# Expert rows in a one-by-one order, and the bias tables' transfers issued two stages earlier

## The chip, the cores and the metric

The kernel runs on one core of a Trainium2 chip. The core has five engines with a queue of instructions each: TensorE (PE, with its weight loads as PEld), VectorE (DVE), ScalarE (ACT), GpSimd (POOL) and SyncE (SP). They run side by side and meet only at semaphores. Sixteen DMA engines move data between HBM and the core's memory for all of them. The metric is the device time of one execution in microseconds (us), the median over runs.

## The reference: what is computed

One inference step of a two-layer backbone. 128 context tokens and 512 latent tokens, 1024 channels each, are five blocks of 128 tokens (block 0 is the context). For each layer:

```
sh1, sc1, g1, sh2, sc2, g2 = modulation(cond, w_ada, b_ada)
outs = token_mixer(x * (1 + sc1) + sh1, p)         # 12 attention heads in three groups, and a gated MLP
x = layer_norm(ALPHA * x + g1 * merge_groups(outs, ...), ...)
x = layer_norm(ALPHA * x + g2 * peer_ffn(x * (1 + sc2) + sh2, p), ...)
```

`peer_ffn` routes each token, in each of 8 heads, to 16 of 16384 experts. For one head `h` and slot `k`:

```
act = gelu(peer_u[eid] . x)                        # a "u row": 1024 numbers for each token, a dot product
out += gate * act * peer_v[eid]                    # a "v row": 1024 numbers for each token, a weighted sum
```

That is 8 x 16 u rows and as many v rows for each block of tokens, 256 in all, each a gather of 128 x 4 KB = 512 KB from HBM. Five blocks in two layers make 2560 gathers. Attention group B adds a bias by 2-D offset (`nat_rpb`), for which the kernel builds a table in HBM once, before the first latent block.

## The kernel before, in words

The program is a row of stages with a barrier of all engines between them (`end_step`, L370): `step_modulation` (M), `step_input` (I, one block), `step_attend_route` (A, one block). Layer 0 goes M, I0, A0, I1 to I4, A1 to A4; layer 1 the same, and two closing stages. The expert work of a block is spread over later stages, beside their own work: `Experts(L, block, first, heads)` is a share of it. Six A stages (A2, A3 and A4 of each layer) carry a full block, 8 heads and so 256 rows; the last block's 256 rows have a stage of their own near the end (`step_experts_only`). The other stages carry 1 to 5 heads.

**The order of the rows** is one list that all engines walk (`row_order`, L67): first the 16 u rows of head 0, then `turn` u rows and `turn` v rows by turns. The v rows of head h come about one head after its u rows. `turn` is SHORT_TURN = 4 for a full block and 16 for a smaller share. A row goes through these hands:
- POOL gathers row r into slot r % 8 of the ring, once row r - 8 has been used (`gather_until`, L493). POOL issues strictly in the order of the list.
- A u row: DVE takes its dot product with the token (L594). After u row 15 of a head ACT does the gelu of 16 sums (L529); DVE makes the weights `wsel` of the head's v rows from it (L587), just ahead of v row 0.
- An odd v row: DVE adds it to `acc` (L604). An even v row: ACT writes the weight on a diagonal (L536, four buffers), PE multiplies by it into PSUM (L562, on record as four matmuls). `on_pe` (L80) decides.

**Where rows stand in a stage's own work** is set by shares: each engine calls `rows(n)` between pieces of its own work, which carries it to row n of the list. In an A stage, attention head i of 12 stands between `rows(9 i)`, `rows(9 i + 4)` and `rows(9 i + 9)`. In half i, rows 9 i to 9 i + 3 stand right before the head's value products (PE, L1157), for which DVE waits before it scales the result (L1326). DVE's `rows` come before that wait, PE's before those products. Then follow the projection `w_out` (PE L1169, DVE L1360), the routing's projection (PE L1189) and its top 16 (DVE, L1375 to L1390).

**The bias tables** are `bias_rows_gpsimd` (L631), called by POOL at the start of stage A0: 16 transfers from HBM to HBM, which lay out the rows (L638), a wait for them, two loads of the tables into the unused ring (L643), a wait, two additions of the mask (L647), two stores (L650). Behind them in POOL's queue stands the power function for the group norm of A0's attention result (L1273), for which DVE waits (L1355). No expert rows run in M, I0 and A0 of layer 0, so POOL has little to do there.

Of the kernel before, what the change touches and what calls it, by code (L numbers as in the profile page):

```python
# [16 lines left out]
DEPTH, D = 2, 1024  # L17
# [16 lines left out]
PH, PK, TOPK = 8, 128, 16  # L34
# [24 lines left out]
HEAD_ROWS = 2 * TOPK  # L59
BY_PE = 2  # L60
DIAGS = 4
SHORT_TURN = 4

# [8 lines left out]
def row_order(heads, turn):  # L74


    u = [("u", h, k) for h in range(heads) for k in range(TOPK)]
    v = [("v", h, k) for h in range(heads) for k in range(TOPK)]
    order, u = u[:TOPK], u[TOPK:]
    while v:  # L80
        order += u[:turn] + v[:turn]
        u, v = u[turn:], v[turn:]
    return order


def on_pe(kind, k):
    return kind == "v" and k % BY_PE == 0


class Experts:  # L90
# [7 lines left out]
    def __init__(self, layer, block, first, heads, begin=False, end=False, ended=None):  # L98
        self.layer, self.block, self.first, self.heads = layer, block, first, heads
        self.begin, self.end, self.ended = begin, end, ended  # L100
        self.order = row_order(heads, SHORT_TURN if heads == PH else TOPK)

        self.by_dve, self.by_pe = [], []
        d = p = 0
        for kind, _, k in self.order:
            if on_pe(kind, k):
                p += 1
            else:
                d += 1
            self.by_dve.append(d)  # L110
            self.by_pe.append(p)

        self.before = block * PH + first + layer * (NBLK * PH)
# [10 lines left out]
def build(nc, a):  # L124
    es = ExitStack()
    with es:
# [5 lines left out]
        def sem(name):  # L132
            s = es.enter_context(nc.semaphore(name))
            sems.append(s)
            return s
# [150 lines left out]
        pieces_used = sem("pieces_used")  # L286
# [6 lines left out]
        const_in = sem("const_in")  # L293
# [78 lines left out]
        def chain(eng, s):  # L372

            n = [0]

            def link(ins):
                n[0] += 1
                ins.then_inc(s, 1)
                eng.wait_ge(s, n[0])
            return link  # L380
# [54 lines left out]
        def last_sum_rstd(pool):  # L435
            pool.wait_ge(end_var, 1)
            pool.tensor_tensor(rstde[:, :], vee[:, :], neg_half[:, 0:1], ALU.pow).then_inc(end_rstd, 1)
# [7 lines left out]
        def experts_gpsimd_ended(pool, E):  # L445
            if E is not None and E.ended is not None:
                last_sum_rstd(pool)
# [174 lines left out]
        natmask = x2e[:, 0:GRID_W]  # L622
# [5 lines left out]
        def start_sync_more(sp):  # L628
            sp.dma_start(iota16[:, :], a["c_iota"]).then_inc(cache_in, 16)

        def bias_rows_gpsimd(pool):  # L631

            pool.dma_start(natmask, a["c_natmask"]).then_inc(const_in, 16)
            for l in range(DEPTH):
                for h in range(H):
                    for half in range(2):
                        first = ((l * H + h) * (2 * NA_KH - 1) + 1 - half) * RPB_ROW + RPB_PAD + NA_KW - 1
                        pool.dma_start(toep_dram[l, half * GRID_W:(half + 1) * GRID_W, h * NDR * GRID_W:(h + 1) * NDR * GRID_W]  # L638
                                       .rearrange("p (r c) -> r p c", c=GRID_W),
                                       bass.AP(a["rpb"].tensor, first, [[RPB_ROW, NDR], [-1, GRID_W], [1, GRID_W]])).then_inc(bias_stored, 16)  # L640
            pool.wait_ge(bias_stored, 16 * DEPTH * H * 2)
            for l in range(DEPTH):
                pool.dma_start(toepf[l], toep_dram[l, :, :]).then_inc(const_in, 16)  # L643
            pool.wait_ge(const_in, 16 * (1 + DEPTH))
            for l in range(DEPTH):
                t = toepf[l].rearrange("p (r c) -> p r c", c=GRID_W)
                pool.tensor_tensor(t, t, natmask.unsqueeze(1).broadcast_to([P, H * NDR, GRID_W]), ALU.add).then_inc(const_done, 1)  # L647
            pool.wait_ge(const_done, DEPTH)
            for l in range(DEPTH):
                pool.dma_start(toep_dram[l, :, :], toepf[l]).then_inc(bias_stored, 16)  # L650
# [6 lines left out]
        def step_modulation(L, E, first=False):  # L657
# [10 lines left out]
            with nc.Block() as block:  # L668
# [84 lines left out]
                @block.gpsimd  # L753
                def _(pool):
                    rows, finish = experts_gpsimd(pool, E)
                    experts_gpsimd_ended(pool, E)
                    for c in range(ADA_PIECES):
                        rows((c + 1) * SHARE)
                    finish()
# [30 lines left out]
        def step_input(L, b, context, weights, E):  # L790
# [4 lines left out]
            with nc.Block() as block:  # L795
# [129 lines left out]
                @block.gpsimd  # L925
                def _(pool):
                    link = chain(pool, pool_chain)
                    rows, finish = experts_gpsimd(pool, E)

                    def rope(out, src, nh, stride, half, first, tabs):  # L930

                        w = 2 * half
                        s4 = src.rearrange("p (h n) -> p h n", h=nh)
                        o4 = out.rearrange("p (h n) -> p h n", h=nh)
                        t4 = ropeA[:, 0:nh * w].rearrange("p (h n) -> p h n", h=nh)
                        u4 = ropeB[:, 0:nh * w].rearrange("p (h n) -> p h n", h=nh)
                        cos = rope_t[:, tabs:tabs + w].unsqueeze(1).broadcast_to([P, nh, w])
                        sin = rope_t[:, tabs + w:tabs + 2 * w].unsqueeze(1)
                        pool.tensor_tensor(u4, s4[:, :, first:first + w], cos, ALU.mult)
                        pool.tensor_tensor(t4[:, :, 0:half], s4[:, :, first + half:first + w],  # L940
                                           sin[:, :, 0:half].broadcast_to([P, nh, half]), ALU.mult)
                        link(pool.tensor_tensor(t4[:, :, half:w], s4[:, :, first:first + half],
                                                sin[:, :, half:w].broadcast_to([P, nh, half]), ALU.mult))
                        return pool.tensor_tensor(o4[:, :, first:first + w], u4, t4, ALU.add)

                    rows(96)

                    pool.wait_ge(var_done, 1)
                    pool.tensor_tensor(rstd[:, 1:3], ve[:, 1:3], neg_half[:, 0:2], ALU.pow).then_inc(rstd_done, 1)

                    pool.wait_ge(xT_done, 1)
                    pool.wait_ge(z_act, 1)
                    pool.wait_ge(loaded2, 16)
                    rope(kr[:, NOPE:CH], z[:, C_C + QR + KVR:C_D], 1, CH, ROPE // 2, 0, 0).then_inc(rope_done, 1)
                    pool.wait_ge(rope_done, 1)
                    pool.wait_ge(z_dve, 2)
                    rope(zr, z[:, C_D:C_D + 6 * HD], 6, HD, HD // 2, 0, 2 * ROPE).then_inc(rope_done, 1)
                    pool.wait_ge(rope_done, 2)
                    rows(144)

                    pool.wait_ge(var_done, 2)
                    pool.tensor_tensor(rstd[:, 0:1], ve[:, 0:1], neg_half[:, 0:1], ALU.pow).then_inc(rstd_done, 1)
                    rows(176)
                    pool.wait_ge(up_sb, 1)
                    rope(qc, qc, H, CH, ROPE // 2, NOPE, 0).then_inc(qc_roped, 1)
                    finish()

                @block.vector
# [65 lines left out]
        def step_attend_route(L, b, context, weights, E):  # L1034
# [48 lines left out]
            with nc.Block() as block:  # L1083
# [177 lines left out]
                @block.gpsimd  # L1261
                def _(pool):
                    rows, finish = experts_gpsimd(pool, E)
                    if E is None:
                        bias_rows_gpsimd(pool)
                    for i in range(NH):
                        if i == 1:
                            rows(HEAD_MID)
                            experts_gpsimd_ended(pool, E)
                        rows(i * HEAD_SHARE)  # L1270
                    rows(A_END)
                    pool.wait_ge(var_done, 1)
                    pool.tensor_tensor(rstd[:, :], ve[:, :], neg_half[:, :], ALU.pow).then_inc(rstd_done, 1)  # L1273
                    rows(TAIL[0])
                    rows(TAIL[2])
                    pool.wait_ge(var_done, 2)
                    pool.tensor_tensor(rstd[:, 0:1], ve[:, 0:1], neg_half[:, 0:1], ALU.pow).then_inc(rstd_done, 1)
                    for i in range(12):
                        rows(ROUTE[i])
                    if E is None:  # L1280
                        pool.wait_ge(bias_stored, 16 * (DEPTH * H * 2 + DEPTH))
                    finish()
# [320 lines left out]
```

## Time and profile before

| | us |
|---|---|
| median of 3 runs | 5437.8 (5434.72 to 5450.85) |
| profiled execution, its own time | 5450.89 |
| its span in the trace | 5449.1 |
| busy in the span: PE, DVE, POOL, ACT | 3095.8, 3441.4, 2880.5, 630.1 |
| bytes moved | 1664.83 MB, mean 306 GB/s |
| stages (start to start): M, I0, A0 of layer 0 | 107, 52, 208 |
| one full-block A stage | about 471 |

Engines overlap, so busy times do not add up to the span. A stage lasts until its slowest chain is through, since all engines meet at its end. In the rows of waits an arrow names what an engine waited for, and the numbers are the sum, the number of times and the longest.

### The profile page before, as it was taken

The page shows a single profiled execution, that of the slowest core. Times are in us where ns is not written, and L with a number is a line of the kernel's source. Part 1 is how long each engine was busy: PE and PEld are TensorE (multiplying, and loading weights), DVE is VectorE, ACT ScalarE, POOL GpSimd, SP SyncE. Part 2 cuts the span into 40 slices and gives each one's busy share as a digit, 9 for nine tenths or more (in the row PEclk, how much of TensorE's full clock was granted, in tenths as well). Part 3 has the DMA queues.
Part 4 walks back from the last instruction along what each step waited for, and adds up shares of the span by engine and source line. Part 5 has one row for each costly group of instructions (what it writes and reads, how often), then busy time and mean ns, then how long its engine had stood idle before and what let it go on. Part 6 is the DMA issues. An engine that isn't in the chain of part 4 may idle for free. (4 is left out here: it accounts for less than half of the span.)

```text
span 5449.1 us, 35111 instructions
## 1 busy us (share of the span) xinstructions
PE 3095.8 (57%) x9560; PEld 1601.3 (29%) x9560; DVE 3441.4 (63%) x6877; ACT 630.1 (12%) x1577; POOL 2880.5 (53%) x2837
## 2 busy tenths in 40 slices
PE   8446756357455635656555576645664664565454
PEld 2233334134122323411232233422332331232111
DVE  1245556666776856773468455566686677769665
ACT  0100120110021111000010001111111101211000
POOL 0216635366555645654455464435664564666675
PEclk9678858678677767878777787776776786777677
DMA  7537778789888988989888778778998898998998
GB/s 275 184 155 259 243 285 298 277 309 359 325 301 332 344 301 298 367 333 388 306 311 288 292 242 300 267 260 301 340 341 312 298 367 301 326 341 331 356 385 321
DMA packets 438101, 1664.83 MB, mean 306 GB/s; under 512 B 52928, under 2 KB 66304, under 8 KB 427376
## 3 DMA queue, kind: packets, MB, share of 16 engines
q0 software_dynamic: 370528, 1353.39, 67.7%
q1 hardware_dynamic: 67392, 309.32, 14.8%
q8 instruction: 78, 1.28, 0.1%
q14 instruction: 103, 0.84, 0.0%
HBM read 1634.85 MB, written 33.95 MB: 306 GB/s over the span
## 5 line engine op out<-in xcount | busy, mean ns | idle before, releaser
L562 PE MATMUL ps<-ring,diag 128*128 128x512 f32 x2560 | 1559.6, 759 | 1217.4 <-ACT diag L536 786.8
L493 POOL DMA_INDIRECT ring<-in_peer_v,eid_s x1280 | 1365.5, 1067 | 1038.3 <-PE ps L562 444.8
L493 POOL DMA_INDIRECT ring<-in_peer_u,eid_s x1280 | 1339.2, 1046 | 875.3 <-DVE dots L594 529.3
L594 DVE CUSTOM_DVE_ANT_0 ring<-ring,ps 128x1024 f32<-128x1024 f32 x1104 | 1305.8, 1217 | 121.1 <-DMA ring<-in_peer_u,eid_s 110.2
L562 PEld LDWEIGHTS ps<-ring,diag 128*128 128x128 f32 x2560 | 581.9, 242 | 2050.9 <-issue 1338.1
L604 DVE SCALAR_TENSOR_TENSOR acc<-ring,wsel,acc 128x1024 f32<-128x1024 f32 x640 | 827.1, 1292 | 486.0 <-DMA ring<-in_peer_v,eid_s 438.7
L852 PE MATMUL ps<-W,hT 128*128 128x512 f32 (+1 forms) x800 | 321.6, 563 | 31.2 <-DVE hT L978 22.0
L536 ACT ACTIVATE diag<-ident,wsel 128x128 f32<-128x128 f32 x640 | 225.2, 395 | 706.6 <-DVE wsel L587 392.2
L1189 PEld LDWEIGHTS ps<-hT,W 128*128 128x128 f32 x2560 | 294.7, 193 | 32.3 <-issue 17.7
L1189 PE MATMUL ps<-hT,W 128*128 128x128 f32 x2560 | 296.8, 277 | 11.6 <-ACT hT L1245 11.6
L594 DVE CUSTOM_DVE_ANT_0 ring<-ring,x2e 128x1024 f32<-128x1024 f32 x176 | 219.2, 1281 | 87.1 <-DMA ring<-in_peer_u,eid_s 85.9
L1137 PE MATMUL ps<-ktB,xs 64*128 64x512 f32 x64 | 49.3, 1130 | 316.3 <-DMA xs<-spill_state 179.5
L852 PEld LDWEIGHTS ps<-W,hT 128*128 128x128 f32 x800 | 150.5, 202 | 191.3 <-issue 166.0
L735 PE MATMUL ps<-W,condS 128*2 128x512 f32 x384 | 173.4, 612 | 41.1 <-DMA toep<-in_b_ada 41.1
L1300 DVE SCALAR_TENSOR_TENSOR big<-ps,toep 128x512 f32<-128x512 f32 x32 | 22.0, 689 | 256.4 <-DMA band<-in_c_band 213.9
L1152 PE MATMUL ps<-ident,big 128*128 128x128 f32 x504 | 107.1, 353 | 133.6 <-ACT big L1228 133.6
L484 POOL COPY eid_s<-eid_e 128x16 uint32<-128x16 uint32 (+1 forms) x80 | 17.9, 224 | 298.7 <-DMA eid_e<-expert_ids 211.5
L529 ACT ACTIVATE gel<-dots 128x16 f32<-128x16 f32 x80 | 17.2, 216 | 1362.8 <-DVE dots L594 1316.8
L1326 DVE TENSOR_SCALAR aux<-ps,small 128x64 f32<-128x64 f32 x120 | 34.1, 284 | 188.9 <-PE ps L1157 186.7
L1169 PE MATMUL ps<-W,hT 128*128 128x512 f32 x320 | 142.2, 600 | 1.1 <-ACT hT L1240 1.1
L1152 PEld LDWEIGHTS ps<-ident,big 128*128 128x128 f32 x504 | 81.5, 184 | 183.1 <-ACT big L1228 142.5
L1235 ACT COPY big<-ps 128x512 f32<-128x512 f32 x96 | 56.3, 586 | 597.3 <-PE ps L1152 597.3
(206 smaller groups left out, 2848.6 us busy)
## 6 DMA issues: line engine op xcount, KB each, us to landing
W<-in_w_q SPq DMA_DIRECT2D x28, 2048.0 KB
W<-in_w_ada SPq DMA_DIRECT2D x24, 2048.0 KB
W<-in_w_out SPq DMA_DIRECT2D x10, 4096.0 KB, 27.0
W<-in_w_in SPq DMA_DIRECT2D x16, 2048.0 KB, 8.1
ring<-in_peer_u,eid_s POOLq DMA_INDIRECT x1280, 6.3
ring<-in_peer_v,eid_s POOLq DMA_INDIRECT x1280, 6.1
toep<-mod_rows SPq DMA_DIRECT2D x20, 512.0 KB, 7.6
aux<-mod_rows SPq DMA_DIRECT2D x19, 512.0 KB, 5.9
```

What stands on the lines that cost most here:

```text
L493: pool.indirect_dma_start(ring[:, r % RING, :], None, a["peer_u"] if kind == "u" else a["peer_v"], bass.IndirectOffsetOnAxis(ap=eid_s[:, h ...
L536: act.activation(diag[:, n % DIAGS, :], ident[:, :], ACT.Copy, scale=wsel[:, h % 2, k:k + 1]).then_inc(diag_done, 1)
L562: last = pe.matmul(acc_ps[:, c * 512:(c + 1) * 512], diag[:, (E.by_pe[r] - 1) % DIAGS, :], ring[:, r % RING, c * 512:(c + 1) * 512], start ...
L594: dve.tensor_tensor_reduce(out=ring[:, r % RING, :], in0=ring[:, r % RING, :], in1=x2, scale=1.0, scalar=0.0, op0=ALU.mult, op1=ALU.add, a ...
L604: dve.scalar_tensor_tensor(acc[:, :], ring[:, r % RING, :], wsel[:, h % 2, k:k + 1], acc[:, :], ALU.mult, ALU.add).then_inc(used_dve, 1)
L735: last = pe.matmul(bank(c % NB, parts=2), condS[:, k, :], ada[:, c % NB, k, :], start=(k == 0), stop=(k == KD - 1))
L852: last = pe.matmul(bank(c, n), hT[:, k, :], w_in[c][:, k, :], start=(k == 0), stop=(k == KD - 1))
L1137: pe.matmul(near(i, lat), q, k[:, k0 * P:k0 * P + lat], start=True, stop=True)
L1152: last = pe.transpose(into, pr[:, i % 2, s * P:(s + 1) * P], ident[:, :])
L1169: last = pe.matmul(bank(2 + c), hT[:, k, :], w_out[:, k, c * 512:(c + 1) * 512], start=(k == 0), stop=(k == KD - 1))
L1189: last = pe.matmul(bank(2 + i % 2)[:, g * P:(g + 1) * P], w_q[c][:, k, g * P:(g + 1) * P], hT[:, k, :], start=(k == 0), stop=(k == KD - 1))
L1235: act.copy(prT[:, i % 2, 0:lat], near(i, lat))
```

## The change

Two things. In a full block the two kinds of row alternate one by one behind the first 16 (`turn` 1 for 4). And `bias_rows_gpsimd` is cut in three: the 16 transfers are issued in the first modulation stage once 8 of its 12 weight pieces have been used; the mask's load, the wait for the 16, and the table loads go to the front of POOL's queue in I0, with the wait for these at its end; the additions and stores stay at the start of A0.

```
-SHORT_TURN = 4
...
-        self.order = row_order(heads, SHORT_TURN if heads == PH else TOPK)
+        self.order = row_order(heads, 1 if heads == PH else TOPK)
...
-        def bias_rows_gpsimd(pool):
-
-            pool.dma_start(natmask, a["c_natmask"]).then_inc(const_in, 16)
+        def bias_rows_begin(pool):
+
+            pool.wait_ge(pieces_used, 8)
             for l in range(DEPTH):
                 for h in range(H):
                     for half in range(2):
...
                         pool.dma_start(toep_dram[...], bass.AP(a["rpb"]...)).then_inc(bias_stored, 16)
+
+        def bias_rows_load(pool):
+
+            pool.dma_start(natmask, a["c_natmask"]).then_inc(const_in, 16)
             pool.wait_ge(bias_stored, 16 * DEPTH * H * 2)
             for l in range(DEPTH):
                 pool.dma_start(toepf[l], toep_dram[l, :, :]).then_inc(const_in, 16)
-            pool.wait_ge(const_in, 16 * (1 + DEPTH))
+
+        def bias_rows_end(pool):
+
             for l in range(DEPTH):
...
                     experts_gpsimd_ended(pool, E)
+                    if first:
+                        bias_rows_begin(pool)
...
+                    if E is None:
+                        bias_rows_load(pool)
                     rows(96)
...
                     rope(qc, qc, H, CH, ROPE // 2, NOPE, 0).then_inc(qc_roped, 1)
+                    if E is None:
+                        pool.wait_ge(const_in, 16 * (1 + DEPTH))
                     finish()
...
                     if E is None:
-                        bias_rows_gpsimd(pool)
+                        bias_rows_end(pool)
```

**POOL, first stages.** In the program before, POOL's queue at the start of A0 of layer 0:

```order
L1261 UNCONDITIONAL_BRANCH
L633 DMA x2e<-in_c_natmask 128x64
L638 DMA bias_rows<-in_rpb 14x64x64 x16
L643 DMA ring<-bias_rows 128x3584 x2
L647 TENSOR_TENSOR ring<-ring,x2e 128x3584 x2
L650 DMA bias_rows<-ring 128x3584 x2
L1273 TENSOR_TENSOR rstd<-ve,neg_half 128x4
```

Now, from the first modulation stage into I0 (the row `L369 ISA` is the barrier between them), up to the first power function of I0:

```order
L637 DMA bias_rows<-in_rpb 14x64x64 x16
L673 UNCONDITIONAL_BRANCH
L369 ISA
L932 UNCONDITIONAL_BRANCH
L643 DMA x2e<-in_c_natmask 128x64
L646 DMA ring<-bias_rows 128x3584 x2
L958 ISA
L958 TENSOR_TENSOR rstd<-ve,neg_half 128x2
```

And at the start of A0, now:

```order
L1272 UNCONDITIONAL_BRANCH
L652 TENSOR_TENSOR ring<-ring,x2e 128x3584 x2
L655 DMA bias_rows<-ring 128x3584 x2
L1284 TENSOR_TENSOR rstd<-ve,neg_half 128x4
L1288 TENSOR_TENSOR rstd<-ve,neg_half 128x1
```

The small transfers left A0 for M, the table loads left it for I0; ahead of A0's first power function stand two additions and two stores.

**ACT, a full-block A stage**, around the gelu of expert head 1 and the exponentials of attention heads 6 and 7. Before:

```order
L536 ACTIVATE diag<-ident,wsel 128x128 x2
L529 ACT_TABLE_LOAD
L529 ACTIVATE gel<-dots 128x16
L536 ACTIVATE diag<-ident,wsel 128x128
L1226 ACT_TABLE_LOAD
L1226 ACTIVATE big,small<-ps,small 128x512
```

Now:

```order
L535 ACTIVATE diag<-ident,wsel 128x128
L528 ACT_TABLE_LOAD
L528 ACTIVATE gel<-dots 128x16
L535 ACTIVATE diag<-ident,wsel 128x128 x2
L1237 ACT_TABLE_LOAD
L1237 ACTIVATE big,small<-ps,small 128x512
```

Before, the diagonal behind the gelu is that of v row 12 of head 0. Now all diagonals of head 0 stand ahead of the gelu, and the two behind it are v rows 0 and 2 of head 1.

**DVE, the same stage**, in attention head 9, at the weights of expert head 2 (`wsel`), up to the scaling of the attention result. Before:

```order
L594 ISA ring,dots<-ring,ps 128x1024
L594 ISA dots 128x1
L594 ISA ring,dots<-ring,ps 128x1024
L594 ISA dots 128x1
L594 ISA ring,dots<-ring,ps 128x1024
L594 ISA dots 128x1
L594 ISA ring,dots<-ring,ps 128x1024
L594 ISA dots 128x1
L587 TENSOR_TENSOR wsel<-gel,gates_e 128x16
L1323 TENSOR_TENSOR small<-small 128x1
L1324 RECIPROCAL small<-small 128x1
L1326 TENSOR_SCALAR aux<-ps,small 128x64
```

Now:

```order
L603 SCALAR_TENSOR_TENSOR acc<-ring,wsel,acc 128x1024
L593 ISA ring,dots<-ring,ps 128x1024
L593 ISA dots 128x1
L586 TENSOR_TENSOR wsel<-gel,gates_e 128x16
L593 ISA ring,dots<-ring,ps 128x1024
L593 ISA dots 128x1
L603 SCALAR_TENSOR_TENSOR acc<-ring,wsel,acc 128x1024
L593 ISA ring,dots<-ring,ps 128x1024
L593 ISA dots 128x1
L1334 TENSOR_TENSOR small<-small 128x1
L1335 RECIPROCAL small<-small 128x1
L1337 TENSOR_SCALAR aux<-ps,small 128x64
```

The weights came last before the scaling, behind four dot products; now three rows of DVE's own stand between the weights and the scaling.

## Rows read from the trace of the kernel before

The rows of busy time (Rows 1 and 6) give the stretch and its length, then the busy time of each engine with its count of instructions, then PE's granted clock as a share of full speed, the DMA engines' busy share and the rate.

**Rows 1.** I0, A0, A, experts alone: PE, PEld, DVE, ACT, POOL; clock, DMA, GB/s.
```profile
107.00:159.00 52.00, 39.52 (x125) 20.98 (x125) 10.48 (x35) 5.56 (x11) 7.00 (x14) 0.86 0.23 72
159.00:367.00 208.00, 75.92 (x396) 57.93 (x396) 76.57 (x288) 17.44 (x52) 33.01 (x25) 0.62 0.38 141
1460.50:1932.00 471.50, 256.80 (x824) 137.46 (x824) 331.62 (x655) 61.74 (x152) 270.37 (x267) 0.75 0.88 324
...
5281.00:5321.00 40.00, 20.04 (x30) 7.66 (x28) 27.59 (x39) 2.88 (x9) 30.83 (x31) 0.74 1.01 378
```

**Rows 2.** POOL in order of time, I0 and A0 (start, length; in brackets idle before).
```profile
134.07 0.71 POOL L949 TENSOR_TENSOR rstd<-ve,neg_half 128x2 f32<-128x2 f32 x1 [133.62 <-DVE ve L993]
...
160.78 12.14 POOL L638 DMA_DIRECT2D bias_rows<-in_rpb  x15
207.16 0.82 POOL L638 DMA_DIRECT2D bias_rows<-in_rpb  x1 [34.24 <-issue]
...
222.85 15.41 POOL L647 TENSOR_TENSOR ring<-ring,x2e 128x3584 f32<-128x3584 f32 x2 [10.80 <-DMA ring<-bias_rows]
...
239.68 1.05 POOL L1273 TENSOR_TENSOR rstd<-ve,neg_half 128x4 f32<-128x4 f32 x1
```

**Rows 3.** Waits in the first 330 us (sum, times, longest).
```profile
DVE aux L1355 <- POOL rstd L1273: 30.3, 1, 30.3
...
DVE aux L1348 <- DMA xs<-in_x: 14.0, 1, 14.0
```

**Rows 4.** DMA queues of A0: 159 to 212 us, then 212 to 222.
```profile
q1 hardware_dynamic: 1840, 12.65, 61.5%
q0 software_dynamic: 1312, 3.71, 24.8%
...
q0 software_dynamic: 283, 3.67, 95.4%
```

**Rows 5.** SP in M: the last weight piece, the last load.
```profile
68.90 0.35 SPq L676 DMA_DIRECT2D W<-in_w_ada  x1
...
104.22 0.32 SPq L712 DMA_DIRECT2D modr<-mod_rows  x1
```

**Rows 6.** Busy time in M, 85 to 100 us, columns as in Rows 1.
```profile
85.00:100.00 15.00, 11.33 (x27) 2.12 (x25) 1.36 (x2) 0.00 (x0) 0.00 (x0) 0.99 0.84 314
```

**Rows 7.** Waits of DVE in a full-block A stage, 1460 to 1932 us.
```profile
DVE aux L1326 <- PE ps L1157: 25.2, 7, 5.1
```

**Rows 8.** DVE in attention heads 5 to 9 of that stage.
```profile
1586.34 0.28 DVE L1326 TENSOR_SCALAR aux<-ps,small 128x64 f32<-128x64 f32 x1 [5.03 <-PE ps L1157]
...
1602.72 0.28 DVE L1326 TENSOR_SCALAR aux<-ps,small 128x64 f32<-128x64 f32 x1 [4.55 <-PE ps L1157]
...
1629.36 0.28 DVE L1326 TENSOR_SCALAR aux<-ps,small 128x64 f32<-128x64 f32 x1
...
1647.18 0.28 DVE L1326 TENSOR_SCALAR aux<-ps,small 128x64 f32<-128x64 f32 x1 [5.06 <-PE ps L1157]
```

**Rows 9.** PE in that stage (four matmuls are one v row).
```profile
1606.78 1.98 PE L562 MATMUL ps<-ring,diag 128*128 128x512 f32 x4 [0.40 <-DMA ring<-in_peer_v,eid_s]
...
1642.37 3.52 PE L562 MATMUL ps<-ring,diag 128*128 128x512 f32 x4 [4.16 <-ACT diag L536]
...
1746.53 3.75 PE L562 MATMUL ps<-ring,diag 128*128 128x512 f32 x4 [13.67 <-ACT diag L536]
```

**Rows 10.** DVE behind the attention heads of that stage.
```profile
1718.59 1.23 DVE L1360 TENSOR_TENSOR aux<-ps,aux 128x1024 f32<-128x1024 f32 x1 [2.82 <-PE ps L1169]
...
1752.23 1.28 DVE L604 SCALAR_TENSOR_TENSOR acc<-ring,wsel,acc 128x1024 f32<-128x1024 f32 x1 [6.44 <-DMA ring<-in_peer_v,eid_s]
```

**Rows 11.** POOL's gathers by line, full-block A stage (busy, mean ns | idle before).
```profile
L493 POOL DMA_INDIRECT ring<-in_peer_v,eid_s x128 | 135.2, 1056 | 108.0 <-PE ps L562 50.7 <-issue 25.0 <-DVE acc L604 22.5
L493 POOL DMA_INDIRECT ring<-in_peer_u,eid_s x128 | 131.3, 1026 | 75.8 <-DVE dots L594 45.7 <-issue 26.2 <-POOL eid_s L484 2.1
```

**Rows 12.** Waits of POOL in the experts-only stage, 5070 to 5430 us.
```profile
POOL ring L493 <- issue: 70.1, 229, 0.5
```

## The prediction

> **What bounds the kernel now.** I read the table of busy times by stage first, since all engines meet at each stage's end and an average over the span hides that the stages have different limits. The reader sees three kinds [rows 1]. In M the DMA engines are busy 0.84 of the time near its end [rows 6]. In A0 nothing is busy: 208 us with a DMA share of 0.38. The full-block A stages last 471 us at a DMA share of 0.88, with DVE busy 332 of 471 us; where the experts run alone the DMA share is 1.0. So the order of the rows can win only in the six full-block A stages, from the 12% in which the DMA engines rest, 0.12 x 471 = 57 us in each.
>
> Second I read POOL's timeline and the waits in A0. POOL issues 15 of the small transfers in 12.14 us, then stands 34.2 us before the 16th, waits for the table loads, adds the mask for 15.4 us, and only then comes to the power function [rows 2]. DVE waits 30.3 us for that, with nothing else to do, and 14.0 us just before for a load of x that is late in a full queue [rows 3]. This is on the path that sets the stage's end.
>
> Third I read the waits of one full-block A stage. DVE idles 25.2 us in 7 of 12 attention heads for PE's value products [rows 7]. POOL idles 50.7 us until PE has used a slot of the ring, 45.7 us for dot products and 22.5 us for sums [rows 11].
>
> **The bias part, A0.** What goes from POOL's queue there: 16 issues, two waits, two loads. What stays ahead of the power function are the additions, 15.4 us, and the issue of two stores; begun at 160, that is over before 180. DVE asks for the function at 239.7 + 1.05 - 30.3 = 210.4 [rows 2, 3], so the 30.3 us go whole. What is late next is the load of x. In A0 the hardware queue used 61.5% of 53 us, 32.6 us of all 16 engines, and the small transfers 24.8%, 13.1 us. The latter go; the stores, of the size of the table loads (3.67 MB, 95.4% of 10 us, 9.5 us), now fall into this stretch [rows 4]. From 160.5 that makes 160.5 + 32.6 + 9.5 = 202.6. x came in a few short DVE operations ahead of 210.4, at about 208.7, so 6 us later than that. Gain: 30.3 + 6 = 36 us; ends: 25 (the additions slow down beside DVE's heads and the stores delay x) and 44.3 (both waits whole).
>
> **The bias part, M and I0.** The 16 transfers start when piece 8 is used, at about 69 us, where SP's own trigger stands [rows 5]. From there to 104 the queue of weights uses 0.84 of the engines [rows 6], 0.84 x 35 = 29.4 us; with 13.1 it is 42.5 us of work in 35, so 7.5 us too much. All of it delays M only if the weights pay; part falls into I0, where the DMA share is 0.23 [rows 1]. The lower end is 0. The upper end is the stand before the 16th issue: if it is again 34.2 us, POOL reaches M's barrier at 69 + 12.1 + 34.2 + 0.8 = 116.1, against I0's start at 107 [rows 1, 2], so 9 us. I take 5. Behind POOL's new wait in I0 stand the power function and the rotations, first wanted at 134 [rows 2]; the transfers are through by 116 in any case, and the table loads take 10 us in an idle DMA. I0 costs 0. The bias part in sum: -36 + 5 = -31 us (ends -44 and -16).
>
> A rule speaks against this move. The Trainium skill, DMA: Bandwidth & Descriptors, Queues, rings and completion order, says that each DMA engine takes packets from its queues by turns. Were those turns of equal time, the small transfers would be through after 13.1 / 0.5 = 26 us, well before M's end, and all of the 7.5 us would fall on the weights instead of 5. The trace shows 61.5 to 24.8 in A0, not equal time [rows 4]. By the rule the part would come to -28.5.
>
> **The order, what it costs on each engine.** Nothing is added. In 8 rows DVE has 4 dots and 2 sums in either order, and every sum waits for the DVE row before it in either; PE has 2 rows in either. What moves is where they stand.
>
> *Attention heads.* With turns of four, the four rows before a head's value products hold 0, 1 or 2 PE rows; now exactly 1, with 3 for DVE. A PE row takes 1.98 us at the full clock and 3.5 to 3.75 us at the lower one [rows 9], a DVE row up to 1.28 [rows 10]. The waits follow this: at 1629.36, four u rows and no PE row, DVE does not wait. The three near 5 us, 14.6 of the 25.2, have a further cause [rows 8]. Head 5: the diagonals of v rows 12 and 14 stand behind the gelu, which needs u row 15. Heads 6 and 9: v row 0's weights come behind four dots, and DVE has little or nothing left while ACT, PE and the products follow. The first cause is gone in the new order. For head 9 the 5.06 us hold that whole chain, with a PE row of 3.52. In the new order DVE has three rows, 3.7 us, beside it: a wait of 1.4, and none at the full clock, for 5.06. Against it: v row 0 of head 0 is now the last row of the half before, with a further PE row to follow, and head 6 has three PE rows; I count 4 to 5 us of wait in each of these two, and 1 us in each of five or six others at the lower clock. That is 15 us where 25.2 were: -10. DMA and ring give back half, since a DVE that is sooner meets rows that have not landed. I take -5 per stage; ends: -25 (all waits gone) and +17 (below).
>
> *Behind the heads.* PE stands 13.67 us for a diagonal behind a gelu; the slot comes free late, and DVE then waits 6.44 us for the v row that lands late [rows 9, 10]. In the new order these diagonals stand ahead of the gelu: -4 of the 6.4. Against that, the last PE row before each half of `w_out` is now the sixth of eight, not the third: 3 rows later, at 256 rows in 471 us up to 5.5 us. DVE waits 2.82 us there already [rows 10], so part of it counts: +3. In the top 16, DVE is busy nearly all the time and its work is the same: 0.
>
> Per stage -5 - 4 + 3 = -6, in six stages -36. The experts-only stage: POOL's main idle time is 229 gaps of 0.3 us between two issues, for which no row in use is to blame, and the DMA share is 1.0 [rows 1, 12]: 0, ends -5 and +3. The small shares keep turns of 16: 0.
>
> **The sum.** 5450.9 - 31 - 36 = 5383.9 for an execution like the profiled one, whose span of 5449.1 is all but 1.8 us of its time. It lies 13.1 us above the median of the runs, 5437.8, within their spread. Against the median: 5437.8 - 67 = 5371.
>
> **The rivals.**
> - *The order moves nothing (0.28).* The A stages carry 256 rows of 0.5 MB and some 18 MB beside them at a DMA share of 0.88; if the idle DMA time is that of chains which do not touch rows (start of stage, norms), only the bias counts: 5437.8 - 31 = 5407. For it: POOL's waits are short and many. Against it: the near 5 us waits recur in all six stages.
> - *The order wins far more (0.12).* If the 50.7 us for PE's slots [rows 11] mostly go and DMA fills them, -20 per stage: 5437.8 - 31 - 120 = 5287. Against it: the bytes of a stage in 20 us less would need a DMA share of 0.88 x 471 / 451 = 0.92 on average, start and norms included.
> - *Slower: PE at the lower clock sets the head (0.12).* Now each head has a PE row right before its products. The granted clock of the stage is 0.75 on average; if it falls with PE's work spread more evenly, each costs 3.5 to 3.75 us, and the five heads without a wait get one of 3.4 us: +17 per stage, 5437.8 - 31 + 102 = 5509. It decides when more than half of the PE rows in the heads take over 3 us; at +5 per stage the kernel is where it was.
> - *The bias part gives nothing (0.03).* If M ends 9 us later, I0 waits for the 16th transfer, and x stays late, some 15 us are left: 5437.8 - 15 - 36 = 5387. It moves the time little.
> - The forecast, in a broad sense (-2 to -14 per stage): 0.45.
>
> **How the numbers follow.** The forecast's own range is 5437.8 - 44 - 84 = 5310 to 5437.8 - 16 - 12 = 5410. I cut half of the far rival below and most of the slower one: 5302 to 5436. A measurement of this kernel can tell about 0.3%, 16 us, from no change. Below 5421 lie the forecast, the far win, the rival without bias and most of the one in which the order moves nothing; 0.8. Within 16 us lie the milder cases of the slower rival, where a loss of 3 to 8 us per stage eats the bias part, and the weak end of the neutral one: 0.11. Slower needs more than +8 per stage: 0.09.
>
> **What would show it.** A0: the wait of DVE L1366 (before: L1355) for the power function gone, the stage near 172 us for 208; the wait for x a few us shorter. M: 107 to 116 us, I0 as before, 52. Full-block A: about 465 us for 471; DVE's waits for value products 15 us for 25, none over 5 at head 5; PE's wait of 13.67 gone, DVE's wait at the projection longer than 2.82. Experts alone: as before. I am wrong if the A stages are longer than 471, if PE's granted clock falls below 0.7 there, or if A0 keeps over 190 us since something else was due at that time.

## The result, and the profile after

The changed kernel is slower: 5457.7 us median of 14 runs against 5439.7 for the kernel before, a ratio of 1.0034 (95% interval 1.0023 to 1.0046). The forecast was 5371, the range ended at 5436. The kernel after was profiled in an execution of 5476.1 us, 18 above its median, the kernel before in one of 5450.9, 11 above its own, so the two traces differ by some 7 us more than the medians do.

The stages say where it went, in us, from one stage's first load to the next's (for the full-block A stages the mean of six, and in it the mean of each part):

| | before | after |
|---|---|---|
| M, I0, A0 of layer 0 | 108.2, 51.2, 208.0 | 118.4, 51.7, 174.2 |
| full-block A: to the scaling of the 12th head | 216.2 | 211.8 |
| ... from there to the end of the norm (input of the routing) | 58.4 | 61.5 |
| ... to the first product of the routing's projection | 24.5 | 29.7 |
| ... to its last score | 46.5 | 51.5 |
| ... to the end | 125.1 | 124.9 |
| full-block A, whole | 470.7 | 479.4 |
| experts alone, with the last sum | 397.7 | 397.0 |

**A0 and M.** POOL in the kernel after, in order of time (start, length, idle before), and with it SP's last load of M:

```profile
69.62 12.33 POOL L637 DMA_DIRECT2D bias_rows<-in_rpb  x15 [69.17 <-PE ps L740]
110.81 0.32 SPq L717 DMA_DIRECT2D modr<-mod_rows  x1
113.33 0.82 POOL L637 DMA_DIRECT2D bias_rows<-in_rpb  x1 [31.37 <-issue]
118.46 0.59 POOL L643 DMA_DIRECT2D x2e<-in_c_natmask  x1 [4.31 <-issue]
...
144.66 0.71 POOL L958 TENSOR_TENSOR rstd<-ve,neg_half 128x2 f32<-128x2 f32 x1 [24.54 <-DVE ve L1004]
...
170.08 15.43 POOL L652 TENSOR_TENSOR ring<-ring,x2e 128x3584 f32<-128x3584 f32 x2 [5.80 <-POOLq L369]
185.81 1.17 POOL L655 DMA_DIRECT2D bias_rows<-ring  x2 [0.30 <-POOL ring L652]
216.02 1.04 POOL L1284 TENSOR_TENSOR rstd<-ve,neg_half 128x4 f32<-128x4 f32 x1 [29.04 <-DVE ve L1362]
```

The additions are over 30 us before the power function is wanted, and POOL now waits for DVE where DVE waited for POOL [rows 2, 3]. DVE's wait for the function fell from 30.3 to 1.2 us, that for the load of x from 14.0 to 8.4:

```profile
DVE aux L1359 <- DMA xs<-in_x: 8.4, 1, 8.4
DVE aux L1366 <- POOL rstd L1284: 1.2, 1, 1.2
```

The stand before the 16th issue moved along: 31.4 us, and with it POOL reached M's barrier last. Two things lengthen M. The last load is issued at 110.8 us and not at 104.2 [rows 5], 6.6 later. And I0's first load follows it after 7.2 us and not after 3.6, since the barrier waits for POOL, whose 16th issue is over at 114.15. Stage by stage, after (columns as in Rows 1):

```profile
0.00:118.00 118.00, 87.36 (x203) 17.76 (x203) 11.17 (x20) 1.50 (x2) 13.34 (x20) 0.93 0.85 324
118.40:170.00 51.60, 39.90 (x125) 21.12 (x125) 10.38 (x34) 5.56 (x11) 8.65 (x17) 0.86 0.40 144
170.00:344.00 174.00, 76.29 (x396) 58.19 (x396) 76.61 (x288) 17.44 (x52) 18.17 (x6) 0.64 0.32 126
1444.10:1920.80 476.70, 268.30 (x824) 140.85 (x824) 332.44 (x655) 62.00 (x152) 274.70 (x267) 0.73 0.87 321
```

In the full-block stage the engines run as many instructions as before, at nearly the same granted clock (0.73 for 0.75); DVE's busy time is the same within 1 us and the DMA share fell from 0.88 to 0.87. PE's busy time rose from 256.8 to 268.3 us, but that is not what the stage pays for: the mixed order below has 264.8 in a stage of 459.9. The stage is longer because something stands.

**What stands.** PE at the routing's projection, after (L1200 is the projection, four pieces, on record as two halves of 32 matmuls each; L561 the v rows; L1188 the transposes of the routing's input):

```profile
1732.79 3.78 PE L561 MATMUL ps<-ring,diag 128*128 128x512 f32 x4 [16.66 <-DMA ring<-in_peer_v,eid_s]
1738.73 3.74 PE L561 MATMUL ps<-ring,diag 128*128 128x512 f32 x4 [2.17 <-ACT diag L535]
1742.28 1.07 PE L1188 MATMUL ps<-ident,aux 128*128 128x128 f32 x8
1744.51 3.84 PE L1200 MATMUL ps<-hT,W 128*128 128x128 f32 x32 [1.16 <-ACT hT L1256]
1748.18 1.88 PE L561 MATMUL ps<-ring,diag 128*128 128x512 f32 x4
1749.90 3.73 PE L1200 MATMUL ps<-hT,W 128*128 128x128 f32 x32
1754.70 1.96 PE L561 MATMUL ps<-ring,diag 128*128 128x512 f32 x4 [1.07 <-ACT diag L535]
1756.49 3.73 PE L1200 MATMUL ps<-hT,W 128*128 128x128 f32 x32
```

and ACT beside it:

```profile
1753.67 0.59 ACT L1260 COPY aux<-ps 128x512 f32<-128x512 f32 x1 [8.92 <-PE ps L1200]
1754.15 0.69 ACT L535 ACTIVATE diag<-ident,wsel 128x128 f32<-128x128 f32 x2
1765.55 0.59 ACT L1260 COPY aux<-ps 128x512 f32<-128x512 f32 x1 [10.71 <-PE ps L1200]
```

The same place before:

```profile
1760.85 3.84 PE L1189 MATMUL ps<-hT,W 128*128 128x128 f32 x32 [1.16 <-ACT hT L1245]
1764.52 3.60 PE L562 MATMUL ps<-ring,diag 128*128 128x512 f32 x8
1767.96 7.31 PE L1189 MATMUL ps<-hT,W 128*128 128x128 f32 x64
1775.10 3.67 PE L562 MATMUL ps<-ring,diag 128*128 128x512 f32 x8
```

Before, two v rows follow a piece's first half and none its second: the four rows there were all u rows. Now one row follows each half. The diagonal of the row behind the second half stands in ACT's queue behind the copy of the piece, and ACT waits with the copy until PE has finished it. So at each piece's end PE stands for a copy and a diagonal, 1.07 us, four times per stage, 4.3 of the 5.0 us; ACT slept 9 to 11 us ahead of each copy with the diagonal's inputs in hand. The second place is above: the v row that PE must take ahead of the transposes (L1188) is row 145 now, expert head 4's first, where it was row 142.

### The profile page after: what moved, and what is told of

Same layout as the page of the kernel before. It is cut to its first block and busy times, and to the rows that moved or that the text cites. A ratio compares the mean times of both kernels' runs of the same rounds, so it can differ in the third digit from the quotient of the medians.

```text
span 5474.3 us, 35178 instructions
## 1 busy us (share of the span) xinstructions
PE 3174.8 (58%) x9560; PEld 1608.2 (29%) x9560; DVE 3443.2 (63%) x6877; ACT 633.0 (12%) x1577; POOL 2875.9 (53%) x2837
## 5 line engine op out<-in xcount | busy, mean ns | idle before, releaser
L561 PE MATMUL ps<-ring,diag 128*128 128x512 f32 x2560 | 1618.2, 776 | 1239.3 <-DMA ring<-in_peer_v,eid_s 685.3
L593 DVE CUSTOM_DVE_ANT_0 ring<-ring,ps 128x1024 f32<-128x1024 f32 x1104 | 1320.1, 1217 | 411.7 <-DMA ring<-in_peer_u,eid_s 405.4
L561 PEld LDWEIGHTS ps<-ring,diag 128*128 128x128 f32 x2560 | 564.9, 239 | 2098.1 <-DMA ring<-in_peer_v,eid_s 1049.6
L1200 PEld LDWEIGHTS ps<-hT,W 128*128 128x128 f32 x2560 | 297.7, 193 | 40.9 <-issue 26.3
L1200 PE MATMUL ps<-hT,W 128*128 128x128 f32 x2560 | 299.8, 277 | 11.6 <-ACT hT L1256 11.6
```

What stands on the lines that cost most here:

```text
L561: last = pe.matmul(acc_ps[:, c * 512:(c + 1) * 512], diag[:, (E.by_pe[r] - 1) % DIAGS, :], ring[:, r % RING, c * 512:(c + 1) * 512], start ...
L593: dve.tensor_tensor_reduce(out=ring[:, r % RING, :], in0=ring[:, r % RING, :], in1=x2, scale=1.0, scalar=0.0, op0=ALU.mult, op1=ALU.add, a ...
L1200: last = pe.matmul(bank(2 + i % 2)[:, g * P:(g + 1) * P], w_q[c][:, k, g * P:(g + 1) * P], hT[:, k, :], start=(k == 0), stop=(k == KD - 1))
```

## The experiments

Ten kernels, each timed in five rounds against the kernel before on the same chip. "Bias part alone" is the changed kernel with turns of four. The parts of a full-block A stage, means of its six stages in one profile, in the order of the table above (heads, to the norm's end, to the projection, to the last score, whole):

| kernel | median us | ratio to before (95%) | heads | norm | to proj. | scores | stage | M |
|---|---|---|---|---|---|---|---|---|
| before | 5440 | | 216.2 | 58.4 | 24.5 | 46.5 | 470.7 | 108.2 |
| after | 5457.7 | 1.0034 (1.0023 to 1.0046) | 211.8 | 61.5 | 29.7 | 51.5 | 479.4 | 118.4 |
| order alone | 5476.0 | 1.0072 (1.0052 to 1.0091) | 208.8 | 62.5 | 29.0 | 51.5 | 476.1 | 108.3 |
| bias part alone | 5407.5 | 0.9944 (0.993 to 0.9958) | 215.5 | 58.3 | 23.9 | 46.5 | 468.9 | 119.8 |
| diagonals ahead | 5411.6 | 0.9957 (0.994 to 0.9973) | 209.0 | 62.0 | 28.4 | 46.3 | 470.3 | 114.8 |
| row 145 behind | 5433.5 | 0.999 (0.998 to 1.0) | 209.2 | 61.8 | 24.2 | 53.7 | 473.3 | 113.9 |
| both | 5412.7 | 0.9947 (0.9929 to 0.9964) | 210.5 | 62.0 | 24.4 | 51.2 | 472.8 | 114.5 |
| mixed order | 5371.5 | 0.9867 (0.9848 to 0.9885) | 209.2 | 57.7 | 24.2 | 46.3 | 462.3 | 117.3 |
| turns of 4, diagonals ahead | 5406.1 | 0.9939 (0.9926 to 0.9953) | 215.4 | 58.3 | 23.9 | 46.7 | 468.7 | 113.7 |
| bias part after piece 1 | 5418.1 | 0.996 (0.9946 to 0.9973) | 216.1 | 58.4 | 24.6 | 46.4 | 470.3 | 120.8 |
| mixed, bias after piece 4 | 5362.9 | 0.9855 (0.984 to 0.9871) | 209.2 | 58.0 | 24.3 | 46.3 | 462.6 | 109.8 |
| mixed, turns of 2 | 5411.4 | 0.9944 (0.993 to 0.9958) | 214.4 | 58.0 | 24.1 | 46.3 | 467.6 | 116.5 |

My theory after the result, the theory of places: the alternating order loses at two places where PE meets a v row right before or after work that others wait for. The rival, the theory of pace: alternating slows gathers and PE throughout, and the two places are only where it shows.

**The two parts, each alone.**

```
-        self.order = row_order(heads, SHORT_TURN if heads == PH else TOPK)
+        self.order = row_order(heads, 1 if heads == PH else TOPK)        # before, with this line alone
```

> The alternating order alone, with the bias transfers where they were in the kernel before. The stages of the two profiles say that the order costs 5 to 9 us in each of the six full-block A stages: expected 30 to 50 us slower than before. Rival: the two parts are not additive (the shift of the bias part moves the phase of everything behind it), and then the order alone is within 10 us of before.

```
-        self.order = row_order(heads, 1 if heads == PH else TOPK)
+        self.order = row_order(heads, 4 if heads == PH else TOPK)        # the changed kernel, with this line alone
```

> The moved bias transfers alone, with turns of four. The first full expert stage started 23 us sooner in the changed kernel (A0 shorter by 34, M longer by 10): expected 20 to 25 us faster than before, 5415 to 5420. My prediction said 31. Rival (not additive): less than 10 us.

The order alone costs 36 us (5476.0 against 5439.9), the bias part alone wins 32 (5407.5). The first was expected (30 to 50), the second won more than the 20 to 25 expected. The sum is +4 against a measured +18. The intervals reach 6, 8 and 11 us to either side, so the 14 us between are at their edge: whether the two parts cost more together than apart stays open. The profiled lengths of M scatter between 114 and 120 us wherever the transfers stand behind piece 8.

**The diagonals ahead of the wait.**

```
                         rows(before(i))
+                        rows(ROUTE[i])
                         act.wait_ge(q_done, i + 1)
                         act.copy(qsel[...], bank(2 + i % 2)...).then_inc(q_sb, 1)
-                        rows(ROUTE[i])
```

> The changed kernel, but in the routing's projection ACT writes the diagonals up to the piece's end before it waits for the piece's products and copies them, not behind. Theory of places: PE's 1.07 us stands for a diagonal behind each piece go, the projection lasts 47 us as before the change and not 51.5, each full A stage is 4 to 5 us shorter, the kernel 25 to 30 us faster than the changed one (about 5430). Theory of pace (alternation slows the gathers and PE everywhere, the stands are only where it shows): the stands go but reappear as waits for landings, under 8 us gained.

46 us faster than the changed kernel, more than expected; the projection is back at 46.3 us. PE in that kernel:

```profile
1745.53 1.88 PE L561 MATMUL ps<-ring,diag 128*128 128x512 f32 x4
1747.25 3.73 PE L1200 MATMUL ps<-hT,W 128*128 128x128 f32 x32
1750.82 1.88 PE L561 MATMUL ps<-ring,diag 128*128 128x512 f32 x4
1752.54 3.73 PE L1200 MATMUL ps<-hT,W 128*128 128x128 f32 x32
```

No stand is left and no wait for landings came in its place, so the first place is shown. From it come 5.2 us a stage, 31 us. The other 15 are not explained by this place. The two profiles, 65 us apart, have the rest in M (3.6), in the heads (2.8 per stage) and ahead of the projection (1.3 per stage), and the heads' part is within what profiles of one order differ by: the seven kernels that alternate in the heads show 208.8 to 211.8 us there, the four with turns of four 215.4 to 216.2.

**Row 145 behind the transposes.**

```
-                    rows(TAIL[3])
+                    rows(TAIL[3] - 4)            # PE, ahead of the wait for x2 and the transposes; ACT likewise
```

> The changed kernel, but PE and ACT go only to row 144 and not to 148 ahead of the transposes of the routing's input, so that row 145, the first v row of head 4, stands behind them. Theory of places: from the end of the norm to the first product of the projection it is 25 us as before the change and not 29.7; 5 us per full A stage, the kernel 25 to 30 us faster than the changed one. Theory of pace: under 8 us gained, since PE then waits for the row behind the transposes.

> Both edits of the two experiments before on the changed kernel: the diagonals ahead of the wait for a piece, and row 145 behind the transposes. Theory of places: the losses stand one behind the other on PE, so the gains add up: 46 + 24 us off 5458 would be about 5390, under the kernel with the bias part alone (5407), since the attention heads' gain of the alternating order is then left over. Rival: the two overlap (a row that waits less at one place waits at the other), and it stays near 5405.

Alone it wins 24 us, and the 5 us ahead of the projection are gone; but with the first edit it wins nothing more (5412.7 against 5411.6). In that kernel PE waits inside the projection for rows that have not landed:

```profile
1733.97 3.60 PE L561 MATMUL ps<-ring,diag 128*128 128x512 f32 x8
1737.41 3.73 PE L1200 MATMUL ps<-hT,W 128*128 128x128 f32 x32
1741.22 1.99 PE L561 MATMUL ps<-ring,diag 128*128 128x512 f32 x4
1743.05 3.73 PE L1200 MATMUL ps<-hT,W 128*128 128x128 f32 x32
1747.35 1.98 PE L561 MATMUL ps<-ring,diag 128*128 128x512 f32 x4 [0.57 <-DMA ring<-in_peer_v,eid_s]
...
1759.01 1.98 PE L561 MATMUL ps<-ring,diag 128*128 128x512 f32 x4 [0.82 <-DMA ring<-in_peer_v,eid_s]
```

The row itself (1.9 us) and the waits moved into the projection: 24.4 and 51.2 us, where it was 28.4 and 46.3. Here the rival is half right, and the 5390 that the theory of places gave did not come. This place has to do with when rows come, and moving PE's part of it moves the loss. A repair must bring the row sooner, which an order in turns of four does by having row 142 as the last and not row 145.

**The mixed order.** Alternate where it wins, take turns where it loses:

```
     while v:
-        order += u[:turn] + v[:turn]
-        u, v = u[turn:], v[turn:]
+        n = 1 if turn == 4 and len(order) < 112 else turn
+        order += u[:n] + v[:n]
+        u, v = u[n:], v[n:]
```

> The bias part as in the change; rows 16 to 111, those of the attention heads, alternate one by one, and from row 112 on they come in turns of four. Theory of places: the heads keep their gain of about 4 us per stage and the two losses are not made: 10 to 25 us faster than the bias part alone, 5385 to 5397. Theory of pace: slower than the bias part alone by the share of rows that alternate, 5415 to 5425.

5371.5 us, 36 faster than the bias part alone and 86 faster than the change, and more than the 5385 to 5397 expected. The heads keep 209.2 us, and each part behind them is as in turns of four. 96 of the 256 rows alternate and cost nothing, so pace is refuted for the heads' stretch. Waits of DVE from a stage's start to the end of its heads, in one stage of this kernel, then in one of the kernel before:

```profile
DVE aux L1338 <- PE ps L1169: 21.9, 8, 5.2
DVE ring L594 <- DMA ring<-in_peer_u,eid_s: 4.3, 4, 1.6
```

```profile
DVE aux L1326 <- PE ps L1157: 25.2, 7, 5.1
DVE acc L604 <- DMA ring<-in_peer_v,eid_s: 4.7, 3, 2.2
DVE ring L594 <- DMA ring<-in_peer_u,eid_s: 3.5, 4, 2.0
DVE acc L604 <- PE ps L556: 2.8, 1, 2.8
```

The value products give 3.3 us here. 4.7 us were waits for v rows in flight, and 2.8 the wait of the first sum for PE's zeroing of its PSUM; both are gone. This stage gained 11 us, more than the mean of 7. The same waits as means of the six stages, with the kernel of turns of two from below:

| DVE in the heads, us | before | order alone | mixed | turns of 2 |
|---|---|---|---|---|
| waits for value products | 23.0 | 21.6 | 21.8 | 21.8 |
| sums: v rows in flight | 5.0 | 0.1 | 0 | 3.7 |
| first sum: PE's zeroing | 2.5 | 0 | 0 | 5.1 |
| dot products: u rows in flight | 2.7 | 2.7 | 3.6 | 1.7 |
| length of the heads | 216.2 | 208.8 | 209.2 | 214.4 |

So the gain of the heads is hardly in the value products, for which the order was changed: it is in the sums of v rows. The zeroing stands in PE's queue with the list's first v row. Where turns of four or two put that row and DVE's first sum (rows 20 and 21, or 18 and 19) into the same half of a head, DVE waits for it, 2.5 us with two dot products between and 5.1 with none; with turns of one (rows 17 and 19) the zeroing is half a head earlier, and DVE does not wait. This is read from the places and the waits; no run moved the zeroing alone.

**Control: the first edit on turns of four.** The same ACT edit as above.

> Control: the bias part alone, in turns of four, with the diagonals ahead of the wait for a piece. With turns of four no PE row stands between a piece's end and the next one's start, so theory of places expects no difference from the bias part alone (within 6 us of 5407). If this edit helps here by 20 us or more, it was no repair of the alternating order but a gain of its own.

5406.1 against 5407.5: no gain of its own. The stand was made by the order.

**How fine the turns must be.**

```
-        n = 1 if turn == 4 and len(order) < 112 else turn
+        n = 2 if turn == 4 and len(order) < 112 else turn
```

> As the mixed order (5371), but in turns of two up to row 111. Theory that what helps the heads is one PE row in each half of a head: turns of two put PE rows at every fourth place too, and the v row of a head comes 2 rows later than with turns of one; gain over turns of four kept in large part, 5371 to 5385, heads' part of the stage 209 to 211 us. Rival: what helps is only that no diagonal stands behind a gelu. In turns of two the diagonal of v row 14 stands behind it again, one for each expert head; then the heads take 213 to 216 us and the kernel about 5395 to 5405.

The rival's numbers came, not its mechanism: heads 214.4 us, as it said, and 5411.4, above even its 5395 to 5405. (The text on record says that a head's first v row comes two rows later than with turns of one; it is one, row 50 for 49 in head 1.) Turns of two also have one PE row in each half of a head, so the balance that I made so much of is worth little by itself. By this trace DVE's mean waits for value products at heads 3, 5, 7, 9 and 11 are 4.4, 2.7, 4.6, 4.3 and 3.9 us, where with turns of one they are 0.2, 0, 1.2, 5.3 and 1.0; but at heads 2, 6 and 10 they are 0, 1.9 and 0, for 6.1, 3.8 and 3.6. The sums are equal, 21.8 us. So the diagonal behind the gelu, which fits head 5's 2.7, is not what the heads lost in sum. What they lost is in the table above: the first sum waits 5.1 us for the zeroing in each of the six stages, and v rows are waited for again. In one of them:

```profile
DVE aux L1338 <- PE ps L1169: 21.8, 6, 4.6
DVE acc L604 <- PE ps L556: 5.1, 1, 5.1
DVE acc L604 <- DMA ring<-in_peer_v,eid_s: 3.5, 4, 1.5
```

**When the bias transfers start.**

```
-            pool.wait_ge(pieces_used, 8)
+            pool.wait_ge(pieces_used, 1)         # turns of four
```

> The bias part alone, in turns of four, with the 16 transfers released after piece 1 of M and not after piece 8. POOL's stand of 31 us before the 16th issue then ends near 65 us, far ahead of the barrier, and the DMA work fits into the idle share of M: M 108 to 110 us and not 119, 5397 to 5400. Rival (the DMA work itself, not the late issue, lengthens M): the weights come later by the same 7 us, and M stays at 115 or more.

```
-            pool.wait_ge(pieces_used, 8)
+            pool.wait_ge(pieces_used, 4)         # mixed order
```

> The mixed order (one by one up to row 111, turns of four behind), with the 16 transfers released after piece 4 of M. After piece 1 the weights came 20 us late, since the queue was still filling the first buffers; after piece 8 POOL's late 16th issue and the weights ran into the barrier. From 40 us on M leaves 0.16 to 0.19 of the DMA engines free, 11 to 13 us, which is what the transfers need: M 108 to 112 us for 117, and 5 to 9 us off the mixed order's 5371. Rival: the transfers cost M their 7 to 10 us wherever they stand: M 115 or more and no gain.

After piece 1 I was wrong and the rival right: M 120.8 us. The 16th issue came at 44.8 us, so it was not what held M; the weights were. (The kernel is 11 us slower than the bias part alone, of which M's 1.0 explains little; the rest is not shown.) In that kernel, waits in the first 120 us:

```profile
PE ps L740 <- DMA toep<-in_b_ada: 20.0, 2, 10.3
```

PE starved twice for a piece (the row names the small load that shares its semaphore). One such wait, of 9.7 us, is in the kernel before too; the second is new. After piece 4 M is 109.8 us, 1.6 over the kernel before, with the bias part's whole gain in A0 kept. POOL in it:

```profile
39.42 12.54 POOL L638 DMA_DIRECT2D bias_rows<-in_rpb  x15 [38.97 <-PE ps L741]
92.51 0.82 POOL L638 DMA_DIRECT2D bias_rows<-in_rpb  x1 [40.56 <-issue]
109.86 0.60 POOL L644 DMA_DIRECT2D x2e<-in_c_natmask  x1 [16.52 <-issue]
```

The stand is still there, 40.6 us, and now ends 17 us before POOL's next work, behind the barrier. At 5362.9 us this is the fastest kernel, 77 us under the one before; its lead over the mixed order (ratios 0.9855 and 0.9867) is inside the intervals, and rests on M's 7.5 us in the profiles.

## Why the prediction was wrong

**The bias part: right in sum, in part by luck.** -31 forecast, -32 measured alone. A0 gave 33.8 us for 36, as argued. M cost 10.2 in the changed kernel and 11.6 with the bias part alone, beyond its upper end of 9, where I took 5. From 69 to 104 us the DMA share was 0.97 and M's last load came 6.6 us late, so most of the 7.5 us of overload fell on M; and the stand before the 16th issue, which I had used only as a bound, came on top with 3.6. I0 cost 0.5. In the profile of the bias part alone the first stage with expert rows starts 20.8 us sooner (346.7 for 367.5), and that is all the terms give. The other 11 of its 32 us lie in the six full-block stages (468.9 for 470.7), which the forecast had left alone; no run shows why.

**The order: -6 per stage forecast, +5.4 measured** (order alone against before; +8.7 in the profile after). By terms:

- Attention heads, -5 forecast: -7.4. Right in sign and near in size, but by luck. The term was -10 for the value products, with half given back to rows that have not landed. The waits for value products fell by 1.4 us (23.0 to 21.6, means of six stages), not by 10: head 5's wait of 5 went and head 2's (5 to 7.5 us) came, both as argued, but head 9 kept its 5 us, where 1.4 or none was argued, and head 10 got a new wait of 2 to 5 us. Landings gave 4.9 us instead of taking 5, and the first sum's wait for the zeroing, of which the forecast said nothing, gave 2.5.
- Behind the heads up to the norm, +3 forecast: +4.1.
- "In the new order these diagonals stand ahead of the gelu: -4 of the 6.4." **This step failed**: +4.5. The diagonals of expert head 3 did come sooner, and PE's stand of 13.67 us for one [rows 9] became one of 16.66 for a row in flight. But the last row that PE takes here, 145, is the first of head 4, and its diagonal does stand behind a gelu, that of u row 142. And the late row behind the 6.44 us [rows 10] did not wait for a slot of PE's: its gather went out at 1740.10, when DVE had used one (the row stands below this list). This is the cause that I did not look for: DVE uses no rows during the norm, the ring's eight slots fill, and gathers go on only when it resumes. What counts is how far beyond the full ring the last PE row ahead of the transposes lies. It was row 142, which landed 16.5 us after DVE had resumed (1755.0 for 1738.55), and is row 145, which landed after 22.0 (1738.0 for 1716.0), one row every 1.3 us. Its diagonal was ready 0.6 us behind the landing. I had counted just these three rows at `w_out` and not here.
- "In the top 16, DVE is busy nearly all the time and its work is the same: 0" was right (125.1 and 124.9 us to the end). But between the norm and the top 16 stands the routing's projection, and the forecast has no term for it. **This is the second failure, +5.0 us per stage**: a PE row now stands at each piece's end, with its diagonal behind a copy that waits for that end. I read PE's and DVE's order there and not ACT's.
- Experts alone: 0 forecast, -0.7.

```profile
1740.10 1.94 POOL L493 DMA_INDIRECT ring<-in_peer_v,eid_s  x1 [6.25 <-DVE acc L604]
```

**The rivals.** The one for slower named another mechanism, PE at the lower clock in the heads; it did not happen: the granted clock of the stage is 0.73 to 0.75, 62 of the 132 PE rows in the six stages' heads took over 3 us (53 before), under the half that was to decide, and the heads are shorter. The chance of slower, 0.09, was too small above all because each place of the stage was weighed for what the order takes away, and only one for what it puts in. The two failed places are off by 8.5 us (+4.5 for -4) and 5.0 per stage, 81 in six, and the other parts of the stage are 2.1 better than forecast, 13 in six: 5371 + 81 - 13 = 5439. The measured 5457.7 is 19 above that. 4 of them are what the order alone costs beyond its stages (36 for 32), and 14 what the two parts cost together beyond their sum; neither is explained.

## What to carry to other kernels

When an order is made finer, look at every place where an engine's own work meets the list, and ask of each engine's queue, the helper's too, what now stands behind a wait that it did not stand behind before. An order that wins in one stretch and loses in another need not be chosen for both: the mixed one kept the gain of the first without the loss of the second. When a forecast of a gain comes true, look whether the waits that were to shrink did: here others did. Background transfers have a best time of their own: started too early they held back weights that PE needed at once, too late they held a barrier, and in between they cost 1.6 us.

## What the runs showed of the hardware

- GpSimd issued 15 of the 224 KB transfers between HBM addresses in 12.1 to 12.5 us and then stood before the 16th for 34.2, 31.4, 13.4 and 40.6 us (before, after, after piece 1, after piece 4). No semaphore stood there. The packets show what the stand lasted for: each transfer is 80 of the 1280 packets, and in each of these kernels the 16th issue began 0.9 to 1.0 us after the 1200th had ended, that is, once all of the first 15 had been moved. After, from 69 us to the issue at 113.3, and after piece 4, from 39 us to that at 92.5:

```profile
q0 software_dynamic: 1200, 3.45, 26.0%
q0 software_dynamic: 1200, 3.45, 21.2%
```

- While both queues had work, the DMA engines' time went to them unequally. From 60 to 118 us the 16 transfers took 21.2% of it, the hardware queue, with the weights, 56.9%:

```profile
q1 hardware_dynamic: 1048, 12.94, 56.9%
q0 software_dynamic: 1280, 3.68, 21.2%
```

- Started after piece 1, the 16 transfers kept PE waiting 10.3 us longer for weights (20.0 for 9.7); started after piece 4, at 39 us, M grew by 1.6 us.
